# Hybrid decoder layer on one core: raw weights summed in place in two sets of buffers, plain products first, the last pair's down operands apart

## The chip, the cores and the metric

The kernel runs on one core of one Trainium2 chip. The metric is the device time of one execution in microseconds (us), and the time given for a kernel is the median of its runs. TensorE does the matrix products into PSUM; DVE is the vector engine, ACT the scalar engine, POOL is GpSimd, and SP issues nearly all DMAs of this kernel. Each engine works through a queue of its own in program order and waits on semaphores.

## The reference, cut to what matters

One layer of a decoder for a prompt of 2048 tokens and 64 sample tokens, in float32. After the mixing layer, every token passes a gated feed-forward network with a norm on each side, and then a gated embedding:

```python
mix = jnp.concatenate([o_g, o_s.astype(x.dtype)], axis=-1) @ w_out
h = x + rmsnorm(mix, w_post_mix)
f = rmsnorm(h, w_pre_ffn)
f = (jax.nn.silu(f @ w_gate) * (f @ w_up)) @ w_down
h = h + rmsnorm(f, w_post_ffn)
h = h + jax.nn.sigmoid(h @ w_ple_gate) * (p @ w_ple_proj)
```

The model width is 1024 and the hidden width of the feed-forward network 2816, which is 22 tiles of 128.

## The kernel before, in words

**Products.** Features lie on partitions and tokens on the free axis. A float32 product is made of three products of rounded parts: every operand x has a large part xh and a small part xl (x minus xh), and TensorE adds wh\*xh, wh\*xl and wl\*xh. ACT makes the large parts (a copy that rounds) and DVE the small ones (a subtraction). The tokens are cut into four chunks; the last, chunk 3, is wide: 512 prompt tokens and the 64 sample tokens, 576 in all.

**Phases.** TensorE's work is a list of units, in phases such as ("z", c), ("out", c), ("ffn", c) and ("ple", c) for chunk c. Here the end of the list matters: out 3, ple 2, ffn 3, ple 3. A unit is one tile of weights. Weights have three slots in SBUF (`wh`, `wl`), and SP loads a unit's weights two units ahead, when the slot's last user is done. Each unit has two parts, and every engine walks the same list of parts: in each part it does the evictions of finished PSUM groups (`evict`), splits of summed weights (`split`, by MAKE, for the unit two further on), the activation (`swish`), the down operands (`late`), and then the steps put beside this part by `beside(kind, chunk, part, step)`. The order on each engine's queue follows from that.

**Seven products.** In ffn 3 the gate and up projections are done by Winograd's form of Strassen's algorithm, which makes a 2 x 2 block product of seven products instead of eight. A pair (`j`, hidden tiles f = 2j and f + 1) is the unit of it. The blocks of weights are A11, A12 (the gate tiles) and A21, A22 (the up tiles), halved along the model width; the blocks of activations are B11, B12, B21, B22, halved along model width and tokens. Four products use sums of weight blocks (S1 = A21 + A22, S2 = S1 - A11, S3 = A11 - A21, S4 = A12 - S2) and four use sums of activations (T1 = B12 - B11, T2 = B22 - T1, T3 = B22 - B12, T4 = T2 - B21). Of the seven units (kind "s", `seven`), A11, A12 and A22 are loaded from DRAM already split, the others are made: SP loads raw weights (step "wraw", 4 DMAs of 512 KB), POOL makes the sums (step "wsum", `weight_sums`), ACT and DVE split them. DVE makes the sums of activations (step "tsum", `operand_sums`), and ACT and DVE split all seven sets once (step "xset", `operand_set`), into buffers that use the regions B, C and R, each free at another time. Products are evicted into four accumulators xs0 to xs3.

**Order.** The order of the seven products is S_X with S_W:

```python
S_X = ["B11", "T2", "T3", "T4", "T1", "B22", "B21"]
S_W = ["A11", "S2", "S3", "A22", "S1", "S4", "A12"]
```

**Buffers.** Raw weights have one set, `raw_g` and `raw_u`; the four sums have buffers of their own, `made`. Raw weights for pair j are asked for beside the first product of pair j - 1, when the last sum of pair j - 1 has been made; each sum waits until the split of the same sum of the pair before is done. Pair 0's raw weights are asked for at part 2 of ple 2, and its sums are made at parts 10 and 18 there.

**Down projection.** Down blocks take four hidden tiles each: after the pairs of f = 4, 8, 12, 16 and 20 comes the down block of the four tiles before, in four units of double length, and after the last of these the block of tiles 20 and 21. `late` writes the down operands of a pair into `gh3` and `gl3`. Every second pair must wait until the down block that reads these places is done.

Of the kernel before, what the change touches and what calls it, by code (L numbers as in the profile page):

```python
# [47 lines left out]
def wide(c):  # L48
    return c == CHUNKS - 1
# [163 lines left out]
for _n, _u in enumerate(UNITS):  # L213
# [290 lines left out]
def build(nc, A, O):  # L504
    ctx = ExitStack()
    with ctx:
# [50 lines left out]
        raw_g, raw_u = [nc.alloc_sbuf_tensor_at(f"raw_{x}", [P, 2, KM * P], f32, offset=raw_at + i * 2 * KM * P * 4)  # L557
# [14 lines left out]
        def put(region, offset, name, shape, dt=f32, over=0):  # L572
# [36 lines left out]
        made = [put("R", 2 * w_, "made1", [P, KM * P]), put("R", 2 * w_ + KM * P * 4, "made2", [P, KM * P])]  # L609
        made += [nc.alloc_sbuf_tensor_at(f"made{3 + i}", [P, KM * P], f32, offset=sq_at + i * 2 * WIDE * 4)  # L610
                 for i in range(2)]

        at = [("B", i * 4 * HW * 4) for i in range(7)] + [("C", i * 4 * HW * 4) for i in range(4)] \
            + [("R", 2 * w_ + 2 * KM * P * 4 + i * 4 * HW * 4) for i in range(3)]
        xh_ = [put(*at[2 * i], f"xh_{x}", [P, 4, HW], f32r) for i, x in enumerate(S_X)]
        xl_ = [put(*at[2 * i + 1], f"xl_{x}", [P, 4, HW], f32r) for i, x in enumerate(S_X)]
        x_raw = {x: put(*at[2 * i + 1], f"xraw_{x}", [P, 4, HW]) for i, x in enumerate(S_X) if x[0] == "T"}
        xs = [put("R", 2 * w_ + 2 * KM * P * 4 + 3 * 4 * HW * 4, "xs0", [P, 2, HW])]
# [102 lines left out]

        def tokens(t):
# [75 lines left out]
        w_sum, wr_in, v_ts, a_xh, v_xl = sem("w_sum"), sem("wr_in"), sem("v_ts"), sem("a_xh"), sem("v_xl")  # L798
        v_sg, v_su = sem("v_sg"), sem("v_su")
# [115 lines left out]
        def _(sp):  # L915
# [170 lines left out]
            def step(what, *a):  # L1086
# [91 lines left out]
        def _(gp):  # L1178
# [99 lines left out]
            def weight_sums(j, which):  # L1278

                lo_, hi_ = slice(0, KM * P // 2), slice(KM * P // 2, KM * P)  # L1280
                a11, a12, a21, a22 = raw_g[:, :, lo_], raw_g[:, :, hi_], raw_u[:, :, lo_], raw_u[:, :, hi_]
                out = [m[:].rearrange("p (e n) -> p e n", e=2) for m in made]
                for i in which:
                    if j:
                        gp.wait_ge(w_lod, RAW_NO[made_unit(j - 1, i)] + 1)
                    if i == 0:
                        gp.wait_ge(wr_in, 64 * (j + 1))
                        if j == 0:
                            gp.wait_ge(gd, GROUP[("proj", 2, KM - 1)] + 1)
                        TT(out[0], a21, a22, ALU.add).then_inc(w_sum, 1)  # L1290
                    elif i == 1:
                        gp.wait_ge(w_sum, made_at(j, 0))
                        TT(out[1], out[0], a11, ALU.subtract).then_inc(w_sum, 1)
                    elif i == 2:
                        if j == 0:
# [1494 lines left out]
```

## Time and profile before

| | |
|---|---|
| median of three runs | 2737.49 us (2736.22 to 2739.92) |
| profiled execution, time | 2743.95 us |
| its span, first to last instruction | 2742.2 us |
| TensorE busy | 2656.9 us, 97% |
| DVE busy | 1366.9 us, 50% |
| ACT busy | 905.7 us, 33% |
| POOL busy | 317.1 us, 12% |
| mean granted clock of TensorE | 0.990 |

These busy shares stand at the head of the profile's page. The busy time of an engine is the sum of its instructions' spans. The granted clock is given as a share of full speed: 1.00 is 2.4 GHz, 0.50 is 1.2 GHz. All times inside the execution are microseconds from the start of the span. ffn 3 starts at 2255.16.

### The profile page before, as it was taken

Reading aid. Unit: us, or ns where it says so; the run is one execution under the profiler, and the core shown is the slowest. Engines: PE = TensorE matmul, PEld = TensorE weight load, DVE = VectorE, ACT = ScalarE, POOL = GpSimd, SP = SyncE. Lnnn points to the kernel's source line nnn. Section 1 sums busy time; section 2 is a strip of 40 time slices with the busy share of each in tenths; the row PEclk is TensorE's granted clock in tenths of the full one; section 3 lists DMA queues with packets and bytes.
Section 4 is the critical chain, followed back from the end, with each engine's and each line's share of the span. In section 5 each row is a group of like instructions: output and inputs, shape, how many; then the busy total and the mean of one; then the engine's idle time right before and its main releaser. Section 6 shows DMA issues by size and latency. Waiting matters only on the chain.

```text
span 2742.2 us, 39069 instructions
## 1 busy us (share of the span) xinstructions
PE 2656.9 (97%) x15096; PEld 2218.9 (81%) x15096; DVE 1366.9 (50%) x2279; ACT 905.7 (33%) x1746; POOL 317.1 (12%) x428
## 2 busy tenths in 40 slices
PE   6999999999999999999999999999999988999998
PEld 4777677777787779987777787777787978999998
DVE  5455552655565673134433566444224576445544
ACT  4345532443334443122222343333122433212122
POOL 0032000111000000001110001111000013233300
PEclk9999999999999999999999999999999999999999
DMA  7865587877777696655544576444445566665554
GB/s 252 315 226 183 197 291 252 270 250 248 235 248 262 226 352 193 224 182 177 177 156 161 206 266 238 168 159 157 158 164 186 193 264 229 215 210 205 185 204 142
DMA packets 226983, 591.40 MB, mean 216 GB/s; under 512 B 27232, under 2 KB 66016, under 8 KB 226400
## 3 DMA queue, kind: packets, MB, share of 16 engines
q1 hardware_dynamic: 226160, 586.80, 61.8%
q8 instruction: 122, 2.00, 0.3%
q0 software_dynamic: 640, 2.10, 0.2%
q14 instruction: 61, 0.50, 0.1%
HBM read 442.34 MB, written 147.65 MB: 215 GB/s over the span
## 4 chain that ended last, share of the span: by engine, by line
PE 85%; DVE 7%; DMA 3%; ACT 2%; issue 2%; SPq 1%; POOL 0%; DVEq 0%; ACTq 0%; POOLq 0%
PE ps L2353 48%; PE ps L2238 19%; PE ps L2268 9%; PE ps L2441 2%; PE ps L2461 1%; DMA wh<-whd 1%; PE ps L2523 1%; PE ps L2561 1%; PE ps L2545 1%; PE ps L2550 1%; DMA wld<-wl 1%; DVE wl L1770 1%; DMA og<-ogd 1%; DVE bl L1931 1%; DVE ssq L1881 1%
## 5 line engine op out<-in xcount | busy, mean ns | idle before, releaser
L2353 PE MATMUL ps<-bh,wh 128*128 128x512 f32 (+1 forms) x1008 | 366.7, 381 | 2.0 <-ACT ta L1383 1.3
L2353 PE MATMUL ps<-bl,wh 128*128 128x512 f32 (+1 forms) x1008 | 361.6, 376 | 0.0
L2353 PE MATMUL ps<-bh,wl 128*128 128x512 f32 (+1 forms) x1008 | 361.2, 375 | 0.0
L2353 PE MATMUL ps<-gh,wh 128*128 128x512 f32 (+1 forms) x880 | 289.8, 362 | 15.3 <-DVE mixF L1805 6.6
L2353 PE MATMUL ps<-gl,wh 128*128 128x512 f32 (+1 forms) x880 | 285.1, 357 | 0.0
L2353 PE MATMUL ps<-gh,wl 128*128 128x512 f32 (+1 forms) x880 | 284.8, 356 | 0.0
L1805 DVE TENSOR_TENSOR mixF<-mixF,ps 128x512 f32<-128x512 f32 (+1 forms) x160 | 112.1, 703 | 237.5 <-PE ps L2353 237.4
L2353 PEld LDWEIGHTS ps<-bh,wh 128*128 128x128 f32 x1008 | 184.6, 189 | 42.7 <-issue 7.0
L2353 PEld LDWEIGHTS ps<-bh,wl 128*128 128x128 f32 x1008 | 185.0, 189 | 36.0
L2353 PEld LDWEIGHTS ps<-bl,wh 128*128 128x128 f32 x1008 | 185.0, 189 | 33.4
L1770 DVE TENSOR_TENSOR wl<-w_raw,wh 128x1024 fp32r<-128x1024 f32 x102 | 125.3, 1229 | 151.9 <-ACT wh L1340 151.8
L2353 PEld LDWEIGHTS ps<-gh,wh 128*128 128x128 f32 x880 | 156.8, 189 | 48.3 <-issue 21.7
L1784 DVE SCALAR_TENSOR_TENSOR tb<-ta,ps 128x512 f32<-128x512 f32 x66 | 45.4, 687 | 282.1 <-ACT ta L1366 282.1
L2353 PEld LDWEIGHTS ps<-gh,wl 128*128 128x128 f32 x880 | 157.1, 189 | 23.7
L2238 PE MATMUL ps<-bh,wh 128*128 128x512 f32 (+1 forms) x640 | 166.2, 398 | 9.2 <-ACT bh L1484 4.7
L2353 PEld LDWEIGHTS ps<-gl,wh 128*128 128x128 f32 x880 | 157.1, 189 | 21.1
L2238 PE MATMUL ps<-bl,wh 128*128 128x512 f32 (+1 forms) x640 | 166.0, 393 | 0.1
L1340 ACT ACTIVATE wh<-w_raw 128x1024 fp32r<-128x1024 f32 x102 | 107.5, 1055 | 164.3 <-PE ps L2353 66.9
L2238 PE MATMUL ps<-bh,wl 128*128 128x512 f32 (+1 forms) x640 | 160.7, 389 | 0.0
L2238 PEld LDWEIGHTS ps<-bh,wh 128*128 128x128 f32 x640 | 117.8, 190 | 40.7 <-issue 4.5
L2238 PEld LDWEIGHTS ps<-bl,wh 128*128 128x128 f32 x640 | 118.1, 190 | 29.8 <-issue 2.9
L2238 PEld LDWEIGHTS ps<-bh,wl 128*128 128x128 f32 x640 | 118.5, 188 | 27.1
(245 smaller groups left out, 4599.6 us busy)
## 6 DMA issues: line engine op xcount, KB each, us to landing
wh<-whd SPq DMA_DIRECT2D x262, 512.0 KB, 3.6
wl<-wld SPq DMA_DIRECT2D x262, 512.0 KB, 4.6
w_raw<-in_w SPq DMA_DIRECT2D x102, 512.0 KB, 4.6
whd<-wh SPq DMA_DIRECT2D x102, 512.0 KB, 5.4
wld<-wl SPq DMA_DIRECT2D x102, 512.0 KB, 6.3
wh<-whd SPq DMA_DIRECT2D x66, 256.0 KB, 3.1
wl<-wld SPq DMA_DIRECT2D x66, 256.0 KB, 4.0
zt<-zd SPq DMA_DIRECT2D x16, 1024.0 KB, 7.6
```

Source lines behind the costliest of these rows:

```text
L1340: A_(wh[s][:], w_raw[s][:], ACT.Copy).then_inc(w_hi, 1)
L1770: V.tensor_tensor(wl[s][:, hb], src[:, hb], wh[s][:, hb].bitcast(f32), ALU.subtract).then_inc(w_lod, 1)
L1784: V.scalar_tensor_tensor(flat(tb[:, 0:w], c), flat(ta[:, 0:w], c), 1.0, acc(g, c), ALU.add, ALU.mult).then_inc(ev[g % 4], 1)
L1805: V.tensor_tensor(flat(mF(c, m), c), flat(mF(c, m), c), acc(g, c), ALU.add).then_inc(ev[g % 4], 1)
L1881: V.tensor_tensor(ssq[:, 0:n], ssq[:, 0:n], sq[k % 2][:, 0:n], ALU.add).then_inc(v_ss, 1)
L1931: V.tensor_tensor(lo[:, k, :], src, hi[:, k, :].bitcast(f32), ALU.subtract).then_inc(a_lo, 1)
L2238: mm = MM(out, ww[SLOT[n]][:, blk * P:blk * P + P], xx[:, k, r_], start=(first and x == kinds[0]), stop=(last_ and x == kinds[-1]))
L2268: mm = MM(acc(g, u.c)[:, hh, :], ww[s][:, at_:at_ + P], xx[i][:, k, :], start=(y == 0), stop=(y == 11))
L2353: last = MM(out, ww[SLOT[n]][:, w_], xx[:, kk, r_], start=(j == 0 and x == 0), stop=(j == len(ks) - 1 and x == 2))
L2441: last = MM(level_bank(r_, l, w)[:, q * 2 * rt:(q + 1) * 2 * rt].rearrange("p (h i) -> p h i", h=2), kd[i % 4][rows(r_), q, 0:w], qd[i % 4 ...
L2461: last = MM(score_bank(m, g), zt[t % 2][rows(g), ZSQ + m, :], kw[t % 2][rows(g), :, :], start=True, stop=True)
L2523: last = TR(key_bank(hf, g)[:, m * P:(m + 1) * P], sc[:, hf, m, g, :], ident[:])
```

## The change

The order of the seven products is changed, so that B11, B22 and B21, plain slices of the normed activations, come first. There are two sets of raw buffers, used in turn; the sums are written over the raw blocks (S1 over A22, S3 over A21, S2 over A11, S4 over A12), and `made` is gone. Raw weights for pair j are asked for beside the last product of pair j - 2, once its S1 is split; pair 0's beside part 1 of out 3, with the sums at part 3; pair 1's beside part 0 of ffn 3, after norm F3. The steps for the activation sets are put in other places. Of the products, ACT now evicts the first two into xs0 and xs1, and DVE the others. The activation (tanh, gate, up) is cut into more steps. The last pair's down operands go into buffers of their own, `gh_last` and `gl_last`, and no longer wait for the down block before them.

```diff
-S_X = ["B11", "T2", "T3", "T4", "T1", "B22", "B21"]
-S_W = ["A11", "S2", "S3", "A22", "S1", "S4", "A12"]
-COMBOS = ["S1", "S2", "S3", "S4"]
+S_X = ["B11", "B22", "B21", "T2", "T3", "T4", "T1"]
+S_W = ["A11", "S4", "A12", "S2", "S3", "A22", "S1"]
+COMBOS = ["S1", "S3", "S2", "S4"]
+T_SUMS = ["T1", "T2", "T4", "T3"]
...
-            if _f % 4 == 0 and _f:
+            if _f % 4 == 0 and 0 < _f < KF - 2:
...
-    beside("ple", 2, 2, "wraw", 0)
-    beside("ple", 2, 10, "wsum", 0, [0, 1])
-    beside("ple", 2, 17, "tsum", 0)
-    beside("ple", 2, 17, "xset", 0)
-    beside("ple", 2, 18, "tsum", 1)
-    beside("ple", 2, 18, "tsum", 2)
-    beside("ple", 2, 18, "xset", 1)
-    beside("ple", 2, 18, "wsum", 0, [2, 3])
-    beside("ple", 2, 19, "tsum", 3)
-    beside("ple", 2, 19, "xset", 2)
-    for i, p in ((3, 1), (4, 3), (5, 5), (6, 7)):
-        beside("ffn", 3, p, "xset", i)
+    beside("out", 3, 1, "wraw", 0)
+    beside("out", 3, 3, "wsum", 0)
+    beside("ple", 2, 16, "xset", 0)
+    beside("ple", 2, 18, "xset", 1)
+    beside("ple", 2, 18, "xset", 2)
+    beside("ple", 2, 19, "tsum", 0)
+    beside("ple", 2, 19, "tsum", 1)
+    beside("ffn", 3, 1, "tsum", 2)
+    beside("ffn", 3, 1, "xset", 3)
+    beside("ffn", 3, 3, "tsum", 3)
+    beside("ffn", 3, 4, "xset", 4)
+    beside("ffn", 3, 6, "xset", 5)
+    beside("ffn", 3, 8, "xset", 6)
     for j in range(1, PAIRS):
-        first = 2 * (OF[GROUP[("s", 3, (2 * j - 2, 0))]] - FIRST[("ffn", 3)])
-        beside("ffn", 3, first, "wraw", j)
-        beside("ffn", 3, first, "wsum", j, [0, 1, 2, 3])
+        part = 2 * (OF[GROUP[("s", 3, (2 * j - 4, 6))]] - FIRST[("ffn", 3)]) if j > 1 else 0
+        beside("ffn", 3, part, "wraw", j)
+        beside("ffn", 3, part, "wsum", j)
...
+        raw_g.append(put("R", 2 * w_, "raw_g1", [P, 2, KM * P]))
+        raw_u.append(nc.alloc_sbuf_tensor_at("raw_u1", [P, 2, KM * P], f32, offset=sq_at))
+
+        def raw_part(j, what):
+
+            raw = raw_u[j % 2] if what in ("A21", "A22", "S1", "S3") else raw_g[j % 2]
+            return raw[:, :, 0:KM * P // 2] if what in ("A11", "A21", "S2", "S3") else raw[:, :, KM * P // 2:KM * P]
...
+        gh_last, gl_last = [put("B", i * 2 * WIDE * 4, f"g_last{i}", [P, 2, WIDE], f32r) for i in range(2)]
...
+        def down_operand(f, i):
+
+            if f == KF - 2:
+                return gh_last[:, :, time_half(3, i)], gl_last[:, :, time_half(3, i)]
+            return gh3[:, f % 4:f % 4 + 2, time_half(3, i)], gl3[:, f % 4:f % 4 + 2, time_half(3, i)]
...
+                    elif j == 1:
+                        sp.wait_ge(v_nm, (NORMS.index("F3") + 1) * KM)
+                        sp.wait_ge(gd, GROUP[("proj", 2, KM - 1)] + 1)
                     else:
-                        sp.wait_ge(w_sum, made_at(j - 1, 3))
+                        sp.wait_ge(w_lod, RAW_NO[made_unit(j - 2, "S1")] + 1)
...
+            def weight_sums(j):
+
+                gp.wait_ge(wr_in[j % 2], 64 * (j // 2 + 1))
+                TT(raw_part(j, "S1"), raw_part(j, "A21"), raw_part(j, "A22"), ALU.add).then_inc(w_sum, 1)
+                TT(raw_part(j, "S3"), raw_part(j, "A11"), raw_part(j, "A21"), ALU.subtract).then_inc(w_sum, 1)
+                gp.wait_ge(w_sum, made_at(j, "S1"))
+                TT(raw_part(j, "S2"), raw_part(j, "S1"), raw_part(j, "A11"), ALU.subtract).then_inc(w_sum, 1)
+                gp.wait_ge(w_sum, made_at(j, "S2"))
+                TT(raw_part(j, "S4"), raw_part(j, "A12"), raw_part(j, "S2"), ALU.subtract).then_inc(w_sum, 1)
...
+                    if i in (2, 4) and m[0]:
+                        dve.wait_ge(v_gl, c * KF + m[0] - (i == 2))
+                    if i == 4:
+                        V.tensor_tensor(xs[1][:, :, :], xs[1][:, :, :], xs[0][:, :, :], ALU.add).then_inc(v_sc12, 1)
+                    pairs = {2: ((2, 0),), 3: ((0, 0),), 4: ((3, 0),), 5: ((0, 3),), 6: ((3, 3), (1, 1))}[i]
...
```

## Rows read from the trace of the kernel before

**Rows 1.** Windows: busy time of each engine, clock, DMA share, GB/s.

```profile
2255.16:2290.10 34.94, 24.27 (x169) 23.86 (x168) 24.48 (x23) 13.21 (x14) 13.26 (x5) 0.90 0.53 184
...
2366.40:2411.40 45.00, 45.00 (x337) 44.80 (x335) 27.07 (x30) 13.29 (x17) 20.64 (x8) 1.00 0.60 200
```

**Rows 2.** Timeline of TensorE: start, length, instruction, idle before it and releaser.

```profile
2222.16 0.47 PE L2353 MATMUL ps<-dh,wh 128*128 128x512 f32 x1 [1.23 <-ACT ta L1383]
...
2229.92 1.24 PE L2372 MATMUL ps<-ssq,mean_r 128*128 128x288 f32 x4 [2.03 <-DVE ssq L1881]
2231.36 0.76 PE L2353 MATMUL ps<-dh,wh 128*128 128x512 f32 x1 [0.20 <-issue]
...
2233.62 0.63 PE L2353 MATMUL ps<-dh,wl 128*128 128x512 f32 x1
...
2265.62 2.26 PE L2268 MATMUL ps<-xh_T,wh 128*128 128x288 f32 x8 [7.10 <-ACT ta L1383]
...
2277.17 1.31 PE L2268 MATMUL ps<-xh_T,wh 128*128 128x288 f32 x8 [3.57 <-issue]
...
2303.08 2.26 PE L2268 MATMUL ps<-xh_T,wh 128*128 128x288 f32 x8 [3.17 <-DMA wh<-whd]
...
2654.97 0.51 PE L2353 MATMUL ps<-gh,wh 128*128 128x288 f32 x2 [2.33 <-DVE gl L1840]
```

**Rows 3.** Waits of TensorE from 2150 on: total us, times, longest.

```profile
PE ps L2353 <- issue: 4.0, 5, 1.5
```

**Rows 4.** Timeline of POOL: the weight sums.

```profile
2211.92 2.69 POOL L1290 TENSOR_TENSOR made<-raw_u 128x1024 f32<-128x1024 f32 x1 [195.88 <-DMA raw_u<-in_w]
...
2254.60 2.85 POOL L1300 TENSOR_TENSOR made<-raw_g,made 128x1024 f32<-128x1024 f32 x1
2275.87 3.84 POOL L1290 TENSOR_TENSOR made<-raw_u 128x1024 f32<-128x1024 f32 x1 [18.42 <-DMA raw_u<-in_w]
...
2399.83 2.40 POOL L1290 TENSOR_TENSOR made<-raw_u 128x1024 f32<-128x1024 f32 x1 [14.01 <-DVE wl L1770]
```

**Rows 5.** Timeline of DVE beside them.

```profile
2212.37 2.78 DVE L1815 SCALAR_TENSOR_TENSOR mixF<-tb,mixF 128x512 f32<-128x512 f32 x1
...
2255.11 3.55 DVE L1858 TENSOR_TENSOR xraw_T<-mixO,xraw_T 128x1152 f32<-128x1152 f32 x1
...
2400.34 2.98 DVE L1770 TENSOR_TENSOR wl<-made,wh 128x1024 fp32r<-128x1024 f32 x1
```

**Rows 6.** By tile: count, duration in ns min/median/max, first and last start.

```profile
L1770 DVE TENSOR_TENSOR wl<-made,wh x44: 1217/1226/2978, 2261.2 to 2614.6; 128x1024 fp32r<-128x1024 f32 x44
...
L1871 DVE TENSOR_TENSOR xl_T<-xraw_T,xh_T x4: 1351/1351/1359, 2260.0 to 2270.0; 128x1152 fp32r<-128x1152 f32 x4
...
L1795 DVE TENSOR_TENSOR xs<-xs,ps x77: 741/749/755, 2271.2 to 2625.8; 128x576 f32<-128x576 f32 x77
```

**Rows 7.** Timeline of ACT at the opening of ffn 3.

```profile
2263.77 1.16 ACT L1501 ACTIVATE xh_T<-xraw_T 128x1152 fp32r<-128x1152 f32 x1 [2.96 <-DVE xraw_T L1863]
2264.84 0.58 ACT L1383 ACTIVATE ta<-ps 128x512 f32<-128x512 f32 x1
```

**Rows 8.** Timeline of SP's queue: raw weights and the load behind them.

```profile
2268.05 0.43 SPq L1138 DMA_DIRECT2D raw_g<-in_w  x1
...
2288.78 0.43 SPq L1138 DMA_DIRECT2D raw_g<-in_w  x1
...
2293.52 0.80 SPq L945 DMA_DIRECT2D wh<-whd  x2
```

**Rows 9.** DMA issues 2146.7 to 2148, in out 3: KB, us to landing.

```profile
wl<-wld SPq DMA_DIRECT2D x1, 512.0 KB, 8.6
```

**Rows 10.** DMA issues 2385 to 2388.5, in a pair.

```profile
raw_u<-in_w SPq DMA_DIRECT2D x2, 512.0 KB, 7.0
```

**Rows 11.** DMA issues 2404.5 to 2406, a down block's first load.

```profile
wl<-wld SPq DMA_DIRECT2D x1, 512.0 KB, 7.4
```

**Rows 12.** DMA issues 2419 to 2421, a later load of that block.

```profile
wl<-wld SPq DMA_DIRECT2D x1, 512.0 KB, 4.4
```

More of the change, by code:

```diff
@@ L607, in build @@
         pjb3 = put("R", 0, "pjb3", [P, KM, WIDE])
[L609 to L618, printed above, removed]
+        raw_g.append(put("R", 2 * w_, "raw_g1", [P, 2, KM * P]))
[3 more added lines that the diff above has]
+            return raw[:, :, 0:KM * P // 2] if what in ("A11", "A21", "S2", "S3") else raw[:, :, KM * P // 2:KM * P]
+        set_size = 4 * HW * 4
+        places = [("B", i * set_size) for i in range(7)] + [("C", i * set_size) for i in range(4)] \
+            + [("R", 2 * w_ + 2 * KM * P * 4 + i * set_size) for i in range(3)]
+        in_order = [(x, h) for x in ("B11", "B22", "B21", "T2", "T1", "T3", "T4") for h in range(2)]
+        place = dict(zip(in_order, places))
+        xh_ = [put(*place[(x, 0)], f"xh_{x}", [P, 4, HW], f32r) for x in S_X]
+        xl_ = [put(*place[(x, 1)], f"xl_{x}", [P, 4, HW], f32r) for x in S_X]
+        x_raw = {x: put(*place[(x, 1)], f"xraw_{x}", [P, 4, HW]) for x in T_SUMS}
+        xs = [put("R", 2 * w_ + 2 * KM * P * 4 + 3 * set_size, "xs0", [P, 2, HW])]
         xs += [nc.alloc_sbuf_tensor_at(f"xs{i}", [P, 2, HW], f32, offset=mixf_at + (i - 1) * 2 * HW * 4)
                for i in (1, 2, 3)]
+        gh_last, gl_last = [put("B", i * 2 * WIDE * 4, f"g_last{i}", [P, 2, WIDE], f32r) for i in range(2)]
         class Scratch:
@@ L1276, in tile @@
                     state(t)
[L1278 to L1295, printed above, removed]
-                            gp.wait_ge(v_nm, (NORMS.index("F3") + 1) * KM)
-                        TT(out[2], a11, a21, ALU.subtract).then_inc(w_sum, 1)
-                    else:
-                        gp.wait_ge(w_sum, made_at(j, 1))
-                        TT(out[3], a12, out[1], ALU.subtract).then_inc(w_sum, 1)
+            def weight_sums(j):
[6 more added lines that the diff above has]
+                TT(raw_part(j, "S4"), raw_part(j, "A12"), raw_part(j, "S2"), ALU.subtract).then_inc(w_sum, 1)
             for k in range(KM):
@@ L1344, in evict @@
                 (m, _), g, c = u.groups[i], G0[n] + i, u.c
-                if u.kind in ("u",) or (u.kind == "dn" and m_block(u) > 0) or (u.kind == "s" and m[1]):
+                if u.kind in ("u",) or (u.kind == "dn" and m_block(u) > 0) or (u.kind == "s" and m[1] > 1):
                     return
@@ L1386, in m_block, with swish @@
                 return u.groups[0][1][0][0] // 4
-            def swish(c, f, i, half):
-                if half:
+            def swish(c, f, i, what):
+                if what != "tanh":
                     return
                 table(TANHS)
-                act.wait_ge(*evicted(GROUP[("s", c, (f, 6 - i))]))
-                if f or i == 0:
-                    act.wait_ge(v_sg, f + 1 - i)
-                A_(ta[:].rearrange("p (e n) -> p e n", e=2), xs[i][:, :, :], ACT.Tanh, scale=0.5).then_inc(a_sig, 1)
+                act.wait_ge(*evicted(GROUP[("s", c, (f, 6 if i else 2))]))
+                if f + i:
+                    act.wait_ge(v_sg, f + i)
+                A_(ta[:].rearrange("p (e n) -> p e n", e=2), xs[2 - i][:, :, :], ACT.Tanh, scale=0.5).then_inc(a_sig, 1)
             def late(c, f):
                 if wide(c):
-                    if f % 4 == 0 and f:
+                    if f == KF - 2:
+                        act.wait_ge(gd, last_operand_use(c))
+                    elif f % 4 == 0 and f:
                         act.wait_ge(gd, GROUP[("dn", c, KM - 1, f // 4 - 1)] + 1)
-                    for i in (1, 0):
-                        act.wait_ge(v_su, f + 2 - i)
-                        A_(gh3[:, f % 4:f % 4 + 2, time_half(c, i)], xs[3 - i][:, :, :], ACT.Copy, scale=0.5
-                           ).then_inc(a_gh, 1)
+                    for i in range(2):
+                        act.wait_ge(v_su, f + 1 + i)
+                        A_(down_operand(f, i)[0], xs[2 + i][:, :, :], ACT.Copy, scale=0.5).then_inc(a_gh, 1)
                     return
@@ L1498, in operand_set @@
                     act.wait_ge(gd, phase_done("out", 3))
-                if at[2 * i][0] == "R":
+                if place[(x, 0)][0] == "R":
                     act.wait_ge(v_pg, 3 * KM)
@@ L2221, in operand @@
                 if u.kind == "dn":
+                    if wide(u.c) and u.groups[0][1][0][0] == KF - 2:
+                        return gh_last, gl_last
                     return (gh3, gl3) if wide(u.c) else (gh, gl)
```

106 lines of the change are left out of this document (62 added, 44 removed).

## The prediction

> **What bounds the kernel now.** The head of the page comes first (the table above): TensorE is busy 97% of the span, so a change can give back only what TensorE waits, and the question is where. The windows by stage answer it for chunk 3: its gate and up projections run in pairs of tiles, seven products a pair, and two undisturbed pairs take 45.00 us [rows 1], 22.5 us a pair or 3.21 us a product. The first pair takes 34.94 us, with TensorE busy for 24.27 and a granted clock of 0.90. The timeline of TensorE gives the places [rows 2]. In the stage before, ple 2, it waits 1.23 and 2.03 us, and the matmuls that follow run at the lower of the two clock levels: from 2231.36 to 2233.62 they start 0.45 us apart (five steps), where 45.00 / 337 x 512 / 288 = 0.24 is the full clock's; some seven of them cost 1.3 us. After product 0 of the first pair it waits 7.10 us, after product 2 another 3.57. Before unit 10 (the fourth product of the second pair) it waits 3.17, and its first eight matmuls take 2.26 us instead of 1.24. The waits by releaser show 4.0 us in five waits at starts of down blocks and the like [rows 3]; the fifth is the 0.20 at 2231.36, so the four at down blocks are 3.8 us. The last down block waits 2.33.
>
> What can be had at most is the sum: ple 2 1.23 + 2.03 + 1.3 = 4.6; first pair 34.94 - 22.5 = 12.4; second pair 3.17 + 1.0 = 4.2; down blocks 3.8; last block 2.3. Together 27.3 us, 1.0% of 2737.
>
> **Why it waits there.** DVE and POOL slow each other [rows 4, 5]. POOL's first weight sums run from 2211.9 on, and DVE's 0.69 us instruction that starts at 2212.37 takes 2.78. The sum of 2254.60 ends at 2257.45; DVE's T2 instruction that starts at 2255.11 takes 3.55, and ends 1.2 us after it, which is its own length. The same at 2400.34: 2.98 us for an instruction of 1.22, beside POOL's sum of 2399.83 to 2402.23. These DVE instructions read two SBUF operands; the evictions, which read PSUM and SBUF, keep to 0.75 beside the same POOL work [rows 6]. In ple 2 POOL makes two sums, and each puts about 2 us (2.78 - 0.69 the first) into DVE's chain of norm F3, for which TensorE then waits. At the first pair, ACT's queue has the large part of T3 ahead of the tanh of the last ple group [rows 7], whose PSUM bank product 1 needs; T3 comes late from DVE. The 3.57 us wait is for the A22 weights, whose load stands in SP's queue behind a wait for the last y store and the 2 MB of pair 1's raw weights. The 3.17 us wait is again for loads behind raw weights and the copies of the caches [rows 8].
>
> The Trainium skill (SBUF — State Buffer, "Who interferes with whom") says the same of that port pair: an exclusive lock for a whole instruction, taken also by a DVE instruction with two SBUF inputs. Were bandwidth shared instead, the turns walked below would cost nothing and the gain would be near 25 us. The trace agrees with the lock.
>
> **The change, part by part.** Durations are those of [rows 6, 7]: a split of weights 1.22 us on DVE, of operands 1.16 on ACT and 1.35 on DVE, an eviction 0.75; a sum on POOL 2.4.
>
> *First sums earlier.* Pair 0's loads and four sums move from ple 2 to out 3. POOL is then silent in ple 2: DVE is some 4 us earlier in a chain late by 2.03, ACT's tanh too, and both waits and the low clock go: -4.6. In out 3 DVE has idle stretches, so the sums hide there; without them they would cost up to the same 4 us. The 2 MB do not hide wholly: SP issues them just before a unit's load, the small part of which now lands after 8.6 us [rows 9] and is needed about 12.5 after its issue. At some 380 GB/s 2 MB add 5.4: 14.0 - 12.5 = 1.5 late, less idle gaps of the DMA engines. I take +1.0 (bounds 0 and 2.5).
>
> *Plain operands first.* B11, B22, B21 need the norm alone, so products 0, 1, 2 follow without a wait, and ACT's queue has only splits ahead of the tanh. That removes the 7.10. A12's load is ahead of raw weights in SP's queue, and A22's is asked for at product 3 and needed at 5; the 3.57 goes too. What is late next? I walk the queues of ACT and DVE in their order of steps, with product 0 starting at 0 and product n needed at 3.21 n; its second kind (small operand) is needed 1.07 later, its third (small weights) 2.14. Before 0 DVE has the norm's last tiles, the evictions of ple 5 and 6 (1.4 each) and the small parts of B11, B22, B21 (1.35 each); that ends at -0.6. Then S4's small weights (0.6), T1 (1.9), T2 (3.2), the last ple group (4.6), T4 (5.9), T2's small part (7.2), S2's (8.4), T3 (9.7); ACT makes T3's large part (10.9), DVE its small part (12.2) and S3's (13.4). The last y is ready at 4.6, so SP issues pair 1's raw weights at 5.0 to 6.9, and POOL can start some 7.8 after the first issue (2268.05 to 2275.87 now), at 12.8. T3's small part at 12.2 and S3's at 13.4 are in time (needed 13.9 and 15.0). Then POOL's sums and DVE take turns: sum 1 13.4 to 15.7; eviction and tanh; T4's large part at 16.0, its small part waits for sum 2 (to 18.0) and is ready at 19.2, needed at 17.1: 2.1 late. The gate product waits for sum 3; T1's small part waits for sum 4 (to 24.5), ready at 25.7, needed at 22.5: 3.2 late. Bounds: 0 where the turns fall well, 4 x 2.35 = 9.4 where all four sums are waited for in full (2.35: 2.40 less what the engines overlap). Neither is near the walk, so I take 5.3 + 0.6 of lower clock = 5.9: -12.4 + 5.9 = -6.5.
>
> *Second pair.* Pair 2's raw weights now wait for S1's split, at about 27, and A12's load is behind them: issued 28.8 with 2 MB just ahead, its 0.5 MB large part lands near 35, needed at 34.3. About 1.0 stays of the 4.2: -3.2 (bounds -4.2 and +3).
>
> *Two sets of buffers, in place.* The same four sums, eleven times. Pair j's raw weights are asked for in pair j-2's last product. Where a down block follows, the sums run inside it, beside evictions that read PSUM: nothing (with splits there instead, 0.8 each as below). Where a pair follows (sums beside pairs 2, 4, 6, 8), 2 MB land 7.0 to 8 us after their issue [rows 10] and POOL starts 4 to 5 us into the pair, just where DVE splits f's gated product, S2 and S3. Undisturbed, S2's small part is ready at 7.4 and needed at 11.8. Walked with turns, it comes at 13.6 if POOL starts at 4.0 (1.8 late) and at 11.8 if it starts at 5.0 (on time). I take 0.8 for each of four: +3.2 (bounds 0 and 9).
>
> *Down blocks.* A block's first load now follows A22's by 6.4 us, not A12's by 3.2. With a load right ahead the small part lands after 7.4 us; alone, after 4.4 [rows 11, 12]; 6.1 is needed. -3.3 of 3.8 (bounds -3.8 and +0.5).
>
> *Last pair's down operands apart.* They are made during the block before, by DVE instructions between its evictions, so the 2.33 goes: -2.3. The tail behind it shifts whole, as its evictions follow TensorE.
>
> *At nothing.* One more ACT eviction a pair (11 x 0.65 us) lies in ACT's idle time (ACT 33% busy). DVE keeps seven instructions a pair for evictions. The semaphores and places cost nothing while no wait binds. If that cover went, they would cost 7 us.
>
> Sum: -4.6 + 1.0 - 6.5 - 3.2 + 3.2 - 3.3 - 2.3 = -15.7 us. The profiled execution took 2743.95 with a span of 2742.2; the median of the runs is 2737.49. The gain is in waits that every run has, so I take it from the median: 2721.8.
>
> **Rivals.**
> *All of it.* The turns fall well, and only 1 to 2 us remain: -25, 2712. For it: in the steady pairs of now DVE was held up (2.98) and TensorE was not. Against: sums now meet splits that TensorE waits for soon.
> *Loads late.* In the five places where a pair follows a pair, A12 comes as late as the load did at 2303: 5 x 4.2 = 21 come back of 27.3, which gives -6, 2731. For it: raw weights stand 4.6 us ahead of that load, 4.74 at 2303's place [rows 8]. Against: the copies of the caches, 1.1 MB, are there only once.
> *Same.* Another wait of equal length at the opening, as T2 to T4 are only moved by three products (9.6 us), and the turns elsewhere take it all: 2737. For it: T3 and T4 still come from the same queue. Against: ACT's queue no longer holds them ahead of the tanh.
> *Slower.* The lock: if all ten pairs paid four turns, 9.4 less the slack of 4.4 (11.8 - 7.4) is 5.0 a pair, 50 in all: 2737 - 27 + 50 = 2760. It decides from 2.7 us a pair. Against: half the sums lie in down blocks.
>
> The Trainium skill (DMA: Bandwidth & Descriptors, "Two DMAs through the same engine are not ordered") has the descriptors of one queue start in order, so that raw weights ahead of A12 are served first; the trace agrees (issued 2293.52 behind them, used 2303.08), and by it alone the time would be that of late loads.
>
> **How the numbers follow.** The forecast (a gain of 10 to 21) has 0.60, all of it 0.14, late loads 0.13, the same 0.06, slower 0.07. Of late loads a fifth would not be told from no change. 0.2% is 5.5 us, about what a measurement of this kernel can tell. So faster 0.85, same 0.08, slower 0.07. The range goes from 2712 (all of it) to 2732 (late loads); 0.04 lie below, and above it the same, slower and 0.03 of late loads, 0.16.
>
> **What the profile after would show.** No POOL work and no wait of TensorE in ple 2; DVE instructions there at 0.7 to 0.8 us. Products 0 to 4 of the first pair without a gap, then waits of 2 and 3 us before the small parts of T4 and T1, beside POOL sums; the first pair 28 to 29 us long. Down blocks without a wait, the last too. What would make it wrong: gaps inside pairs 2, 4, 6, 8, or before A12's product; a wait in out 3 over 3 us; TensorE not idle at T4 and T1, which would make the gain 20 or more.

## The result, and the profile after

The changed kernel takes 2721.61 us (median of four runs, 2719.47 to 2726.8), the kernel before 2738.70 on the same chip (four runs, 2736.22 to 2741.66): a ratio of 0.9935, interval 0.9921 to 0.9948, or 17.1 us. The profiled execution has a span of 2725.0 us, against 2742.2.

Where the 17.2 us of the spans lie is read from four landmarks on TensorE's timeline: the first matmul of out 3, the first of ffn 3, the first of its third pair, and the end. The start of out 3, ahead of everything that the change touches, is 2140.17 before and 2138.59 after. In the fourteen profiled executions of this study it lies anywhere from 2132.45 to 2142.53, so spans are compared from there on.

| stretch, us | before | after | forecast | measured |
|---|---|---|---|---|
| out 3 and ple 2 | 114.99 | 110.59 | -3.6 | -4.4 |
| first pair | 34.94 | 27.72 | -6.5 | -7.2 |
| second pair | 27.26 | 27.41 | -3.2 | +0.2 |
| the rest | 424.84 | 420.69 | -2.4 | -4.2 |
| sum | 602.03 | 586.41 | -15.7 | -15.6 |

The total is that of the forecast, but one row of it is not. A second execution of the changed kernel (After, again, below) has -4.3, -5.9, -3.5 and -3.9 in these four rows, -17.7 in all: the first and the second pair trade with each other from one execution to the next, and the row that misses here is near the forecast there. Windows of the first and second pair of the kernel after, with columns as in [rows 1]:

```profile
2249.18:2276.90 27.72, 24.49 (x170) 23.99 (x168) 24.54 (x19) 10.82 (x12) 10.97 (x4) 0.94 0.74 243
2276.90:2304.31 27.41, 23.88 (x170) 23.68 (x169) 20.72 (x21) 7.71 (x10) 11.50 (x4) 0.94 0.61 213
```

The waits of TensorE after, from out 3 on (releaser, total us, times, longest):

```profile
PE ps L2300 <- DMA wh<-whd: 5.9, 5, 3.5
PE ps L2300 <- DVE xl_T L1901: 3.2, 2, 1.9
PE ps L2385 <- ACT ta L1403: 1.3, 1, 1.3
PE ps L2385 <- issue: 1.0, 1, 1.0
```

Of [rows 3] and of the 7.10, 3.57, 2.03 and 1.23 in [rows 2] nothing is left; the 2.33 before the last down block is gone too. The 1.3 for `ta` stands in ple 3, and stands there before as well. Two kinds have taken the place of the others: operands from DVE, and loads. TensorE's timeline after shows where:

```profile
2159.49 0.50 PE L2385 MATMUL ps<-bh,wh 128*128 128x288 f32 x2 [1.02 <-issue]
...
2268.29 1.45 PE L2300 MATMUL ps<-xl_T,wh 128*128 128x288 f32 x8 [1.91 <-DVE xl_T L1901]
2269.54 2.12 PE L2300 MATMUL ps<-xh_T,wl 128*128 128x288 f32 x8
2271.46 1.81 PE L2300 MATMUL ps<-xh_T,wh 128*128 128x288 f32 x8
2274.59 1.34 PE L2300 MATMUL ps<-xl_T,wh 128*128 128x288 f32 x8 [1.32 <-DVE xl_T L1901]
...
2286.97 2.26 PE L2300 MATMUL ps<-xh_B,wh 128*128 128x288 f32 x8 [3.53 <-DMA wh<-whd]
...
2312.20 1.30 PE L2300 MATMUL ps<-xh_B,wh 128*128 128x288 f32 x8 [1.30 <-DMA wh<-whd]
```

Products 0 to 4 of the first pair run without a gap, then the small parts of T4 and T1 are waited for, as forecast. The 3.53 is product 2 of the second pair, which needs A12; the same product waits 1.30, 0.55, 0.31 and 0.17 in the later pairs that follow a pair. POOL and DVE in the first pair:

```profile
2264.63 2.39 POOL L1311 TENSOR_TENSOR raw_u<-raw_g,raw_u 128x1024 f32<-128x1024 f32 x1
2266.97 3.50 POOL L1313 TENSOR_TENSOR raw_g<-raw_u,raw_g 128x1024 f32<-128x1024 f32 x1
2270.55 2.77 POOL L1315 TENSOR_TENSOR raw_g<-raw_g 128x1024 f32<-128x1024 f32 x1
```

```profile
2264.72 3.52 DVE L1901 TENSOR_TENSOR xl_T<-xraw_T,xh_T 128x1152 fp32r<-128x1152 f32 x1 [1.81 <-ACT xh_T L1522]
2268.16 2.93 DVE L1856 SCALAR_TENSOR_TENSOR tb<-ta,xs 128x576 f32<-128x576 f32 x1
2271.01 0.74 DVE L1825 TENSOR_TENSOR xs<-xs,ps 128x576 f32<-128x576 f32 x1
2271.68 2.86 DVE L1901 TENSOR_TENSOR xl_T<-xraw_T,xh_T 128x1152 fp32r<-128x1152 f32 x1
```

The turns can be followed to 0.2 us. DVE's small part of T4 starts 0.09 after a sum, waits for its end (2267.02) and is done 1.22 later, at 2268.24 (alone it takes 1.35). The next sum, started at 2266.97, waits for that and takes 3.50 instead of 2.40. The gate product then waits for this sum (2270.47), and so on, while the eviction of 2271.01, which reads PSUM, takes 0.74 beside the fourth. This agrees with the rule of the Trainium skill (SBUF — State Buffer, "Who interferes with whom"), by which the loser of the shared ports is blocked and not slowed.

SP's queue in the second pair, and the landing of A12's two halves, from the DMA issues (KB, median us to landing):

```profile
2269.82 0.78 SPq L1147 DMA_DIRECT2D out_k_keep<-in_cache_k  x1
2270.64 0.68 SPq L1148 DMA_DIRECT2D out_v_keep<-in_cache_v  x1
2275.70 0.82 SPq L1164 DMA_DIRECT2D raw_u<-in_w  x2
2276.57 0.90 SPq L1167 DMA_DIRECT2D raw_g<-in_w  x2
2277.59 1.90 SPq L968 DMA_DIRECT2D wh<-whd  x2
```

```profile
wh<-whd SPq DMA_DIRECT2D x2, 256.0 KB, 7.8
```

The raw weights are issued when S1 is split (2275.7), A12's load right behind them at 2277.59; it is used at 2286.97, 9.4 us after its issue.

### The profile page after: what moved, and what is told of

It is laid out like the page before. It is cut to its first block, busy times and chain, and to the rows that moved or that the text cites. A ratio compares the mean times of both kernels' runs of the same rounds, so it can differ in the third digit from the quotient of the medians.

```text
span 2725.0 us, 39082 instructions
## 1 busy us (share of the span) xinstructions
PE 2653.4 (97%) x15096; PEld 2217.6 (81%) x15096; DVE 1388.0 (51%) x2279; ACT 912.6 (33%) x1757; POOL 318.6 (12%) x428
## 4 chain that ended last, share of the span: by engine, by line
PE 86%; DVE 5%; DMA 3%; ACT 2%; issue 1%; SPq 1%; POOL 1%; DVEq 0%; ACTq 0%; POOLq 0%
PE ps L2385 50%; PE ps L2270 20%; PE ps L2300 7%; PE ps L2473 2%; DMA wh<-whd 2%; PE ps L2493 1%; PE ps L2555 1%; PE ps L2593 1%; PE ps L2577 1%; PE ps L2582 1%; DMA wld<-wl 1%; DVE wl L1796 1%; PE ps L2421 1%; ACT wh L1355 1%; DVE mixF L1942 0%
## 5 line engine op out<-in xcount | busy, mean ns | idle before, releaser
L2385 PE MATMUL ps<-gh,wh 128*128 128x512 f32 (+1 forms) x848 | 282.7, 364 | 9.6 <-DVE mixF L1835 7.0
L2385 PE MATMUL ps<-gl,wh 128*128 128x512 f32 (+1 forms) x848 | 278.2, 359 | 0.0
L2385 PE MATMUL ps<-gh,wl 128*128 128x512 f32 (+1 forms) x848 | 278.0, 359 | 0.0
L1810 DVE SCALAR_TENSOR_TENSOR tb<-ta,ps 128x512 f32<-128x512 f32 x66 | 45.4, 687 | 281.1 <-ACT ta L1386 281.1
L2270 PEld LDWEIGHTS ps<-bl,wh 128*128 128x128 f32 x640 | 118.3, 190 | 29.2 <-issue 2.9
```

What stands on the lines that cost most here:

```text
L1810: V.scalar_tensor_tensor(flat(tb[:, 0:w], c), flat(ta[:, 0:w], c), 1.0, acc(g, c), ALU.add, ALU.mult).then_inc(ev[g % 4], 1)
L2270: mm = MM(out, ww[SLOT[n]][:, blk * P:blk * P + P], xx[:, k, r_], start=(first and x == kinds[0]), stop=(last_ and x == kinds[-1]))
L2385: last = MM(out, ww[SLOT[n]][:, w_], xx[:, kk, r_], start=(j == 0 and x == 0), stop=(j == len(ks) - 1 and x == 2))
```

## The experiments

All kernels but the last are the changed kernel with the edit named. The stretches are those of one profiled execution each; "opening" is the first two pairs. Line numbers in a kernel's rows are its own and differ by a few from those of the kernel after. The first four experiments ran on one chip, the next four on another and the last four on a third, each beside the kernel before, whose median there was 2742.07, 2740.48 and 2739.89. The intervals reach 0.001 to 0.0025 to each side, some 3 to 7 us, and a median also holds the time ahead of out 3, which no edit touches. Effects of 1 to 4 us are therefore read from the stretches, and these from one execution each.

| kernel | median us | ratio (95%) | out 3, ple 2 | opening | rest |
|---|---|---|---|---|---|
| before | 2738.70 | 1 | 114.99 | 62.20 | 424.84 |
| after | 2721.61 | 0.9935 (.9921-.9948) | 110.59 | 55.13 | 420.69 |
| sums in ple 2 | 2729.83 | 0.9961 (.9948-.9974) | 114.33 | 56.36 | 420.59 |
| last pair shared | 2729.79 | 0.9957 (.9942-.9972) | 111.36 | 53.95 | 423.64 |
| no sums, pair 1 | 2726.58 | 0.9951 (.9935-.9967) | 110.63 | 54.41 | 422.09 |
| no sums, pairs 1-10 | 2726.50 | 0.9952 (.9934-.9969) | 110.45 | 55.49 | 422.01 |
| sets before tanh | 2721.88 | 0.9937 (.9913-.9961) | 110.66 | 53.37 | 421.10 |
| raw behind load | 2718.93 | 0.9925 (.9906-.9945) | 111.37 | 50.06 | 417.80 |
| cache copies later | 2726.49 | 0.9948 (.9923-.9973) | 110.41 | 54.37 | 420.84 |
| raw 0 behind load | 2721.38 | 0.9935 (.9911-.9959) | 110.28 | 54.19 | 420.98 |
| both behind loads | 2718.34 | 0.9920 (.9907-.9934) | 111.14 | 51.52 | 418.72 |
| after, again | 2724.33 | 0.9945 (.9932-.9958) | 110.67 | 52.79 | 420.91 |
| both, no sums pair 1 | 2713.23 | 0.9908 (.9890-.9926) | 111.09 | 45.62 | 418.60 |
| before, T3 later | 2735.23 | 0.9986 (.9977-.9996) | 114.82 | 63.21 | 423.76 |

**Sums in ple 2.** Does POOL's silence in ple 2 give the 4.6 us? Pair 0's sums are held back to ple 2:

```diff
                 gp.wait_ge(wr_in[j % 2], 64 * (j // 2 + 1))
+                if j == 0:
+                    gp.wait_ge(gd, GROUP[("proj", 2, KM - 1)] + 1)
```

> Pair 0's four sums wait again until the two proj units of ple 2 are done, so POOL works beside DVE's chain of norm F3; all else as in the changed kernel. Theory (POOL's sums hold DVE up and TensorE waits for it): ple 2 gets its waits back, DVE instructions of 2.5 to 3 us beside the sums, the time 4.6 us or more above the changed kernel (four sums are there now, two were before, so up to 8). Rival (the waits in ple 2 came from the 2 MB of raw weights, which stay in out 3 here): no change, ple 2 as long as in the changed kernel within 0.5 us.

The wait for norm F3 is back, with slow matmuls behind it, nearly as in [rows 2]:

```profile
2226.02 2.25 PE L2406 MATMUL ps<-ssq,mean_r 128*128 128x288 f32 x4 [2.00 <-DVE ssq L1913]
```

Out 3 and ple 2 take 114.33 us, 3.7 more than after (4.6 or more was expected), 0.7 less than before. The wait of 1.23 for the tanh does not come back. The step holds.

**Last pair shared.** The down operands of the last pair go back into `gh3` and `gl3`:

```diff
-            if _f % 4 == 0 and 0 < _f < KF - 2:
+            if _f % 4 == 0 and _f:
...
-            if f == KF - 2:
-                return gh_last[:, :, time_half(3, i)], gl_last[:, :, time_half(3, i)]
...
```

> The last pair's down operands are again written into the shared buffers, after the down block before. Theory: the wait of 2.3 us before the last down block is back and nothing else changes, +2.3. Rival (the norm behind it sets the time of the tail, so the wait was hidden or taken elsewhere): 0 to +0.5.

```profile
2642.32 0.51 PE L2379 MATMUL ps<-gh,wh 128*128 128x288 f32 x2 [2.32 <-DVE gl L1866]
```

The rest takes 423.64 against 420.69 and 420.91 in the two executions of the changed kernel: 2.7 to 3.0 more, of which this wait is 2.32. The step holds.

**No sums, pair 1.** Are the waits of 1.91 and 1.32 POOL's turns?

```diff
-                TT(raw_part(j, "S1"), raw_part(j, "A21"), raw_part(j, "A22"), ALU.add).then_inc(w_sum, 1)
+                TT(cut_part(j, "S1"), cut_part(j, "A21"), cut_part(j, "A22"), ALU.add).then_inc(w_sum, 1)
```

with `cut_part` the first 4 columns of each half for j == 1, and the same in the other three sums. The rest of pair 1's sums is left out.

> Pair 1's four sums on POOL are cut to 4 columns of each half, with the same waits; the rest of those sums is left out, so pair 1's made weights are not sums. Theory (turns of DVE and POOL): the waits of 1.91 and 1.32 us at T4 and T1 go, with the slower matmuls behind them, and the first pair takes 22.3 to 22.8 instead of 27.7 us; but the wait of 3.5 in the second pair is for a load and may take some of it. Time -5 to -2. Rival (ACT's queue makes the sets late, not the lock): the waits stay within 0.5 us.

The first pair takes 22.45 us with no wait, and DVE's two small parts 1.36 and 1.35 instead of 3.52 and 2.86. But the opening takes 54.41 us, hardly less than 55.13 and more than the 52.79 of the changed kernel's second execution:

```profile
2286.91 2.26 PE L2305 MATMUL ps<-xh_B,wh 128*128 128x288 f32 x8 [7.37 <-DMA wh<-whd]
```

```profile
wh<-whd SPq DMA_DIRECT2D x2, 256.0 KB, 9.5
```

The turns are real, but the 2 to 5 us expected of the time did not come: removing them gave next to nothing. Counted from the start of ffn 3, A12's load was issued 3.8 us earlier (at 24.6, against 28.4) and used only 1.4 us earlier (at 36.4, against 37.8), and its halves landed after 9.5 us instead of 7.8. Cache copies, raw weights and A12 are in one DMA queue, and an earlier product only waits longer for them.

**No sums, pairs 1 to 10.** The same with all ten pairs' sums cut.

```diff
-        return part[:, :, 0:4] if j == 1 else part
+        return part[:, :, 0:4] if j else part
```

> All sums of pairs 1 to 10 are cut to 4 columns; the rest of them is left out. Theory of the forecast (in pairs 2, 4, 6, 8 DVE and POOL take turns where S2 and S3 are split, 0.8 us a pair): a further -3 against the run with pair 1's sums alone cut. Rival (those waits are for A12's load behind the raw weights): the waits of 1.30, 0.55, 0.31 and 0.17 us stay, no further gain, 0 to -0.5.

```profile
PE ps L2305 <- DMA wh<-whd: 11.6, 5, 7.9
```

With no sum left the five waits before A12's product stay, and the four later ones add up to 3.7 us (2.33 after). So they are not POOL's turns. The rival, loads behind raw weights, is left for these waits.

**Sets before the tanh.** T4 and T1 are split before the first pair's tanh and gate:

```diff
-    beside("ffn", 3, 6, "xset", 5)
-    beside("ffn", 3, 8, "xset", 6)
+    beside("ffn", 3, 5, "xset", 5)
+    beside("ffn", 3, 6, "xset", 6)
```

> The steps that split T4 and T1 stand one and two parts earlier, so ACT makes their large parts before the tanh that waits for product 2's eviction, and DVE's small parts get ahead of POOL's first sum. Theory: the waits of 1.9 and 1.3 us in the first pair go (pair 22.5 to 24), but as in the run without pair 1's sums the second pair's wait for A12's load grows by nearly as much, from 3.5 to 6 or more: net 0 to -2. Rival (the first pair's waits count in full): -4.

```profile
2266.35 1.33 PE L2300 MATMUL ps<-xl_T,wh 128*128 128x288 f32 x8 [1.08 <-DVE xl_T L1901]
...
2270.99 2.29 PE L2300 MATMUL ps<-xh_T,wl 128*128 128x288 f32 x8 [3.32 <-DVE wl L1792]
```

The first pair takes 29.15 us and not the 22.5 to 24 expected. The wait at T4 is gone, another of 0.69 stands before T1's product, and the largest is now for the small part of S1. That part takes its own 1.21 us, but stands in DVE's queue behind instructions that POOL still holds up: T4's small part takes 3.56 there, T1's 3.33, the gate product 2.92. The opening (53.37) lies between the changed kernel's two executions: nothing is won.

**Raw behind load.** Raw weights of pairs 2 to 10 are asked for one unit's load later:

```diff
-        beside("ffn", 3, part, "wraw", j)
+        beside("ffn", 3, part + (2 if j > 1 else 0), "wraw", j)
```

> For pairs 2 to 10 the raw weights are asked for one unit later, so that in SP's queue the load of A12 (of the down block's third unit, where a block follows) stands ahead of them. Theory (A12's load waits behind 2 MB of raw weights, and in the second pair also behind SP's wait for S1's split): the wait of 3.5 us with its slow matmuls and those of 1.30, 0.55, 0.31, 0.17 go, 6 to 7.5 us in all; the first pair keeps its two waits. Rival (the DMA engines are short of time there whatever the order): the waits move to A22's load or to the made weights, gain under 2.

No wait for a load is left in ffn 3, and the two of the first pair stay (1.77 and 2.82), as expected. The opening takes 50.06 us and the rest 417.80, each the least of the kernels so far; the rest is 2.9 less than after, of which the four waits were 2.33. Its median is 2718.93 against 2721.38 to 2726.49 for the other kernels of its chip, with intervals that overlap.

**Cache copies later.** The copies of the caches, 1.1 MB in SP's queue ahead of pair 2's raw weights, move out of the opening:

```diff
-    beside("ffn", 3, 10, "keep")
+    beside("ffn", 3, 46, "keep")
```

> The four copies of caches and last keys, some 1.2 MB, go from the first pair to the first down block. Theory (order in the queue): the second pair's wait falls by what is left of the copies when the raw weights come, from 3.5 to 1 to 2.5, and the small waits of the later pairs stay. Rival (the copies are the cause): 3.5 goes to 0.

```profile
wh<-whd SPq DMA_DIRECT2D x2, 256.0 KB, 5.6
```

```profile
2294.73 1.33 PE L2300 MATMUL ps<-xh_T,wl 128*128 128x288 f32 x8 [2.42 <-DVE wl L1792]
```

A12's halves land after 5.6 us, behind the same raw weights, and in time. With the copies issued some 5 to 7 us ahead of the raw weights, six executions of these kernels show 6.4 to 7.9, and the first two kernels without sums, where they are issued 0.7 us ahead, 9.5 and 9.1. So the copies delay the load, by 0.8 to 2.3 us. That the wait is gone, as the rival had it, does not show more: the first pair is 28.97 us long here, and in the changed kernel's second execution, where it is as long (29.00) and the copies are in place, A12 isn't waited for either. The raw weights land earlier too: POOL's sums start 34.0 us after the start of ffn 3 instead of 36.5, in the midst of DVE's splits, and S2's small part is late, a wait of 2.42 by turns in the place of 3.53 by loads. The opening stays at 54.37.

**Raw 0 behind load.** Pair 0's raw weights one part later in out 3:

```diff
-    beside("out", 3, 1, "wraw", 0)
+    beside("out", 3, 2, "wraw", 0)
```

> Pair 0's raw weights are asked for one part later in out 3, behind the load of a unit instead of before it. Theory: the wait of 1.0 us in out 3 goes, nothing else, -1.0. Rival (2 MB more in that stretch are too much wherever they stand): a wait of 0.5 to 2 us at the next unit.

The wait of 1.02 in out 3 is gone, and another of 0.69 stands further on, as the rival had it, released by ACT:

```profile
2178.62 0.51 PE L2385 MATMUL ps<-bh,wh 128*128 128x288 f32 x2 [0.69 <-ACT mixO L1381]
```

Its chain can be read from the trace. POOL makes pair 0's sums from 2153.01 to 2164.36, and DVE works beside them on the last norm of chunk 2, whose result `mixF` ple 2 needs:

```profile
2156.41 5.68 DVE L1942 SCALAR_TENSOR_TENSOR mixF<-mixF,cols,rs 128x512 f32<-128x512 f32 x2
2162.02 3.48 DVE L1949 TENSOR_TENSOR mixF<-mixF,pjb 128x512 f32<-128x512 f32 x2
```

In the kernel before, with no sum beside them, the same two rows take a quarter and a third of that:

```profile
2162.88 1.41 DVE L1912 SCALAR_TENSOR_TENSOR mixF<-mixF,cols,rs 128x512 f32<-128x512 f32 x2
2164.20 1.29 DVE L1919 TENSOR_TENSOR mixF<-mixF,pjb 128x512 f32<-128x512 f32 x2
```

ACT splits `mixF` into `dh`, and the evictions of out 3 stand behind these splits in its queue. The one that TensorE waits for starts 45.4 us after the first matmul of out 3; the same one started at 39.8 in the kernel before. So this wait is POOL's turns again, read from two traces and not tested by an edit. Out 3 and ple 2 take 110.28 against 110.59. It is not worth a microsecond.

**Both behind loads.** The two edits together.

> The changed kernel with both edits of order in SP's queue together: raw weights of pairs 2 to 10 asked for one unit's load later (behind A12's load), pair 0's one part later in out 3. Theory (these waits are loads that stand behind 2 MB of raw weights, and nothing takes their place): no wait on loads in ffn 3, none of 1 us at the start of the unit in out 3; 5.0 (second pair) + 2.3 (later pairs) + 1.0 (out 3) = 8.3 less than the changed kernel in TensorE's waits, of which executions let some 3 to 6 be seen; time 3 to 6 us under the changed kernel of the same chip, about 2716. Rival (raw weights a unit later bring their sums later, and splits then come late): waits on the small weights of S2 or S3 (released by DVE wl) of 1 us or more in pairs 2, 4, 6, 8, and a time within 1.5 us of the changed kernel's.

Beside the unedited kernel on one chip it is 6.0 us less, 2718.34 (2714.93 to 2718.95) against 2724.33 (2720.81 to 2728.65), and the runs don't overlap. In the stretches from out 3 on the profiled execution is 3.0 us shorter than that of the unedited kernel beside it, and 5.0 shorter than that of the kernel after. A wait of 0.79 for a small weight part is the one new one in ffn 3; out 3 shows 1.21, released by ACT, so only the edit in ffn 3 earns anything. Windows of the first two pairs:

```profile
2246.36:2275.38 29.02, 24.19 (x170) 23.73 (x168) 25.63 (x21) 10.83 (x12) 10.96 (x4) 0.94 0.68 231
2275.38:2297.88 22.50, 22.50 (x170) 22.50 (x169) 16.62 (x18) 6.68 (x9) 10.36 (x4) 1.00 0.69 235
```

The second pair is now an undisturbed one. A12's load has 1.8 us of issue ahead of the raw weights, and its halves land after 2.7 us:

```profile
wh<-whd SPq DMA_DIRECT2D x2, 256.0 KB, 2.7
```

**After, again.** The changed kernel unedited, on the chip of these last kernels.

> The changed kernel once more, unedited, beside the others on one chip: 2719 to 2724, ratio to the kernel before 0.993 to 0.995. It says what the same kernel's waits vary by between two executions (theory: the waits at fixed places stay within 0.3 us, those for loads within 1 us).

The expectation of how little waits vary was wrong. Here the first pair waits 2.82 (T1's small part) and 1.97 (S1's), and takes 29.00. POOL's first sum starts 13.6 us after product 0 and not 13.1, and the turns fall on other instructions: T4's small part takes 1.72, S1's 3.38. A12 isn't waited for at all: its load is issued 0.2 us after the second pair's start and not 0.7, and its halves land after 6.4. The second pair takes 23.79, the opening 52.79, and the later waits are 1.07, 0.62, 0.97. What the first pair loses the second need not lose again, so neither wait has a fixed price.

**Both behind loads, no sums in pair 1.** With loads out of the way, what do the turns cost?

> e10 with pair 1's four weight sums cut to 4 of 1024 columns (that part of the sums is not computed, its operands are then raw weights). With no load late any more behind the first pair, this prices the turns of POOL and DVE alone. Theory (the lock makes T4's and T1's small parts late, and nothing is late behind them): the first pair 22.5 us long with no wait, the second too, and a time 4.5 to 5.5 us under that of e10. Rival (the first pair's lateness would be taken up by something else later, as it was when the loads stood behind): a new wait of 3 us or more in the second pair, and a time within 2 us of e10's.

```profile
2250.18:2272.61 22.43, 22.43 (x169) 22.42 (x168) 19.14 (x20) 10.86 (x12) 0.73 (x4) 1.00 0.79 268
2272.61:2295.80 23.19, 22.70 (x171) 22.49 (x169) 19.33 (x19) 6.67 (x9) 9.21 (x4) 1.00 0.70 257
```

The opening takes 45.62 us, 5.9 less than with the sums, and the medians differ by 5.1 (2713.23; the runs reach from 2709.44 to 2720.83). The same cut gave at most 0.7 while the raw weights stood ahead of A12's load. The turns cost 5 to 6 us, which is seen only with the loads out of the way. It is a price and not yet a gain, as the sums have to be made.

**Before, T3 later.** Is the 7.10 us wait of the kernel before a matter of the queues alone? The kernel before, with T3 behind the tanh of the last ple group:

```diff
-    beside("ple", 2, 19, "tsum", 3)
-    beside("ple", 2, 19, "xset", 2)
+    beside("ffn", 3, 0, "tsum", 3)
+    beside("ffn", 3, 0, "xset", 2)
```

> The kernel before with one edit: the sum T3 and its split stand beside part 0 of ffn 3, behind the tanh of the last ple group, in the queues of DVE and ACT. Theory (the 7.10 us wait was the tanh queued behind T3's large part, but T2, S2 and T3 are themselves late from DVE, so an order of steps alone can't give what the new order of products gave): ACT does the tanh after T2's and S2's large parts, about 2261; product 1 waits some 2.5 to 3.5 instead of 7.10, product 2 then waits 1.5 to 2.5 for T3, the A22 load still comes about 3.5 late (its queue moves up with the last y store); product 3 starts 3 to 4 us earlier than before, and the time is 3 to 4 us less, ratio 0.9985 to 0.999. Rival (the queue order was all of it): product 1 and 2 without a wait over 1 us, and 6 us or more gained. Rival (the order of the steps was not the cause): the 7.10 stays.

```profile
2256.97 2.26 PE L2268 MATMUL ps<-xh_T,wh 128*128 128x288 f32 x8 [2.98 <-ACT ta L1383]
2259.03 2.12 PE L2268 MATMUL ps<-xl_T,wh 128*128 128x288 f32 x8
2260.95 2.12 PE L2268 MATMUL ps<-xh_T,wl 128*128 128x288 f32 x8
...
2269.15 1.59 PE L2268 MATMUL ps<-xh_T,wh 128*128 128x288 f32 x8 [2.79 <-issue]
...
2298.38 2.02 PE L2268 MATMUL ps<-xh_T,wh 128*128 128x288 f32 x7 [5.00 <-DMA wh<-whd]
```

```profile
2250.63:2283.57 32.94, 27.17 (x169) 26.73 (x168) 28.11 (x23) 13.00 (x14) 14.75 (x5) 0.84 0.57 194
```

7.10 becomes 2.98, and product 3 starts 18.5 us after product 0 instead of 22.0, as expected. Product 2 doesn't wait for T3, which had been expected, as product 1 now runs at the lower clock and takes 6 us. Then the gain is lost: 32.94 against 34.94 us for the first pair, with TensorE busy 27.17 against 24.27 at a granted clock of 0.84 against 0.90, and the second pair waits 5.00 for its load, against 3.17. The opening is 1.0 longer than before; the median is 4.7 us less (0.9977 to 0.9996), which the profiled execution doesn't show (601.8 us from out 3 on against 602.0). So the queue order explains 4.1 of the 7.10, but an order of steps alone did not shorten the opening, as the new order of products did.

## Why the prediction was right, and where it was not

*First sums earlier* (-4.6 and +1.0 forecast, -4.4 together measured, against -3.6). Right, mechanism and size: no wait and no POOL work in ple 2, the 1.02 in out 3, and the sums put back bring 3.7 of it back. The +1.0 has a second cause, which the prediction put at nothing ("the sums hide there"): with pair 0's raw weights behind the load its wait is gone, and one of 0.69 or 1.21 appears, which the traces put down to POOL's turns in out 3.

*Plain operands first* (-6.5; -7.2 measured, -5.9 in the second execution). Right: a gap at T4 (1.91, 2.1 forecast) and one at T1 (1.32, in five other executions 2.81 or 2.82, 3.2 forecast). The kernels without sums show that POOL's turns are the cause, and the last of them that these are worth 5.9 us in the opening. That this is the 5.9 of the forecast is in part luck: it was 5.3 of waits and 0.6 of lower clock, and the first pair shows 3.2 of waits and 2.0 of slower matmuls (24.49 busy, against 22.5), in the second execution 4.8 and 1.7.

*Second pair* (-3.2; +0.2 measured, -3.5 in the second execution). In the profiled execution this step failed. It said that A12's load, "issued 28.8 with 2 MB just ahead", lands near 35. It was issued 28.4 after product 0 and used at 37.8, when it had landed, after 9.4 us and not 6.2. The 1.1 MB of cache copies, which the prediction named under a rival and then left out of the sum, are ahead of the raw weights in the queue; with them gone the halves land after 5.6, with them after 6.4 to 7.9. The mechanism was the one named, the size was wrong: the wait went from 3.17 to 3.53, not to 1.0. In the second execution, with a longer first pair, it went to nothing. The forecast gave one price to a wait that has none: of the five executions whose opening no edit changed, three have a first pair of 27.6 or 27.7 us and a second of 26.6 to 28.8, and two have 29.0 or 29.2 and then 23.8 or 24.7. Both pairs together are 5.8 to 9.4 us under the kernel before, where 9.7 were forecast.

*Two sets of buffers, in place* (+3.2; +2.33 measured). Size near, cause wrong: the step put it down to turns at the splits of S2 and S3, and the waits are for A12's load behind the raw weights. They stay when the sums are cut, and go when the load goes first. That is the rival of late loads, which was right in kind in all five places that it named (in three of them in the second execution) and wrong in size: 5.9 us of waits, and not 21. The rule on queues cited in the prediction (the Trainium skill, DMA: Bandwidth & Descriptors, "Two DMAs through the same engine are not ordered") has the descriptors within one queue of one DMA engine start in order. The trace agrees: issued ahead of the raw weights A12's halves land after 2.7 us, behind them after 5.6 to 9.5.

*Down blocks* (-3.3; all 3.8 gone) and *last pair* (-2.3; 2.33 gone). Right. But the 3.8 was read from one execution: in that of the kernel with T3 later, whose down blocks are those of before, the same waits are 0.35, 0.49 and 0.94, 1.8 in all.

So -15.7 against -15.6 is luck in its last digits, and flatters the working: the second pair was 3.4 too good, and the three other stretches together 3.3 too bad (1.8 of it in the rest).

## What to carry to other kernels

When a bulk load becomes due at the same moment as a unit's own load, issue the unit's load first: here one unit's delay of 2 MB took 6 us more off the kernel by the medians, 3 to 5 by the stretches, with no new wait over 0.8 in ffn 3. Before a stall is priced, ask what stands next in line, and look at a second execution of the same kernel: in this opening operands, sums and loads are late by nearly the same amount, and three of the edits moved the wait without shortening it. In a comparison of two traces take the stretches between landmarks, starting where the two kernels are still the same: this removes several microseconds of difference that no edit made.

## What the runs showed of the hardware

A shorter wait can be followed by more slow matmuls than a longer one. After 7.10 us of waiting [rows 2] the groups of eight matmuls took 2.26, 1.65 and 1.23 us; after the 2.98 of the kernel with T3 later 2.26, 2.12, 2.12 and 1.38. In its whole first pair TensorE waited 4.9 us less, and 2.9 came back as busy time (27.17 against 24.27 for the same matmuls), about half of it behind this wait and half behind the next, of 2.79, where 3.57 stood before.

The turns of POOL and DVE stretch POOL too: sums of 2.39 or 2.40 us take 3.50 and 2.77 when a DVE instruction with two SBUF inputs is in turn, so a chain of four sums gets longer by the very instructions that it delays.

What stays open: whether the wait of 0.69 to 1.21 in out 3, released by ACT, goes with pair 0's sums, as the traces say; and how much an order of steps that keeps pair 1's sums off T4's and T1's splits could win of the 5.9 us, as they are due again for pair 1's own second product. Neither was tried.
